# Row sums of a prompt tile in pairs of groups, between the dense blocks of a PEER layer

## What is computed

```python
def one(args):                       # 128 tokens at a time
    xb, ib, gb = args                # x, indices of 8 x 16 experts, their gates
    act = jax.nn.gelu(jnp.einsum("thkd,td->thk", u_tab[ib], xb)) * gb
    return jnp.einsum("thk,thkd->td", act, v_tab[ib])
```

## Time and profile before

| | us |
|---|---|
| median of three runs | 2733.33 |
| the profiled execution | 2734.76 |
| its span in the trace | 2733.0 |
| TensorE busy | 2637.8 (97%) |
| v products of layer 0, from the first to the last | about 995 to 1415 |
| v products of layer 1 | about 2290 to 2720 |

### The profile page before, as it was taken

How to read it: one execution, slowest core, us unless ns; L and a number is a source line. 1 busy time by engine, 2 the same in 40 slices (tenths; PEclk the granted TensorE clock), 3 DMA queues, 4 the chain that set the end, 5 groups by cost and what they waited for, 6 DMA issues and landing times. The chain is left out here.

```text
span 2733.0 us, 39630 instructions
## 1 busy us (share of the span) xinstructions
PE 2637.8 (97%) x15897; PEld 2317.3 (85%) x15897; DVE 1650.5 (60%) x3299; ACT 1035.8 (38%) x1558; POOL 713.1 (26%) x676
## 2 busy tenths in 40 slices
PE   7998799999999999999999889999999999999998
PEld 6997689999999996777779769999999999677775
DVE  3447677888344455555566568987834445555556
ACT  3444332345333332333352653334543333233332
POOL 1001200000111126776723002000011112677773
PEclk9999899999999999999999899999999999999999
DMA  8644476447798869999953123334779896999994
GB/s 302 216 154 150 153 269 218 154 170 282 277 358 310 317 246 362 377 375 384 375 202 109 63 95 115 121 141 187 281 261 355 316 316 243 358 375 386 388 371 183
DMA packets 233109, 704.65 MB, mean 258 GB/s; under 512 B 22112, under 2 KB 154592, under 8 KB 211168
## 3 DMA queue, kind: packets, MB, share of 16 engines
q1 hardware_dynamic: 172912, 516.86, 51.3%
q0 software_dynamic: 59200, 184.79, 18.6%
q10 hardware_dynamic: 816, 0.48, 0.1%
HBM read 598.12 MB, written 103.94 MB: 257 GB/s over the span
## 5 line engine op out<-in xcount | busy, mean ns | idle before, releaser
L1359 PE MATMUL hidden_ps<-h_hi,u_hi 128*128 128x384 f32 x2016 | 681.0, 338 | 2.6 <-issue 1.6
L1359 PE MATMUL hidden_ps<-h_hi,u_lo 128*128 128x384 f32 x2016 | 675.0, 335 | 0.0
L1359 PE MATMUL hidden_ps<-h_lo,u_hi 128*128 128x384 f32 x2016 | 675.0, 335 | 0.0
L2262 DVE TENSOR_TENSOR v_lo<-v_slot,v_hi 128x1024 fp32r<-128x1024 f32 x248 | 304.9, 1229 | 303.8 <-ACT v_hi L2127 302.8
L2127 ACT ACTIVATE v_hi<-v_slot 128x1024 fp32r<-128x1024 f32 x248 | 262.9, 1060 | 545.1 <-PE out_ps L2058 540.3
L2058 PE MATMUL out_ps<-v_hi,act_hi 128*128 128x512 f32 x992 | 395.7, 399 | 10.8 <-DVE act_lo L2272 10.8
L2058 PE MATMUL out_ps<-v_lo,act_hi 128*128 128x512 f32 x992 | 388.8, 392 | 0.0
L2058 PE MATMUL out_ps<-v_hi,act_lo 128*128 128x512 f32 x992 | 387.3, 390 | 0.0
L1359 PEld LDWEIGHTS hidden_ps<-h_hi,u_hi 128*128 128x128 f32 x2016 | 378.9, 188 | 4.7 <-issue 4.7
L1359 PEld LDWEIGHTS hidden_ps<-h_lo,u_hi 128*128 128x128 f32 x2016 | 379.0, 188 | 0.0
L1359 PEld LDWEIGHTS hidden_ps<-h_hi,u_lo 128*128 128x128 f32 x2016 | 378.7, 188 | 0.0
(11 more groups left out here) (502 smaller groups left out, 4009.3 us busy)
## 6 DMA issues: line engine op xcount, KB each, us to landing
u_slot<-in_peer_u SPq DMA_DIRECT2D x64, 2048.0 KB, 9.1
v_slot<-in_peer_v SPq DMA_DIRECT2D x64, 2048.0 KB, 10.2
hidden<-hidden_ring SPq DMA_DIRECT2D x64, 768.0 KB, 6.0
spread_gates<-spread SPq DMA_DIRECT2D x16, 2048.0 KB, 8.2
hidden_in<-hidden SPq DMA_DIRECT2D x64, 512.0 KB
ada_w_ring<-in_ada_w SPq DMA_DIRECT2D x48, 512.0 KB, 6.0
even_w_ring<-in_even_w SPq DMA_DIRECT2D x16, 1024.0 KB, 6.7
ada_w_ring<-in_ada_w SPq DMA_DIRECT2D x16, 1024.0 KB, 6.2
```

Source lines behind the costliest of these rows:

```text
L1359: mm = pe.matmul(PH_[:, b, 0:T], u[:, b, k * P:(k + 1) * P], x[:, k, :], start=(k == 0 and part == 0), stop=(k == KB - 1 and part == 2))
L2262: dve.tensor_tensor(lo, V[o // JC % 2][:, o % JC, :], hi.bitcast(F32), ALU.subtract).then_inc(vl, 1)
```

## The change

The row sums of two neighbouring groups are done at one place. `PAIR_AFTER[k]` = 14 + k\*108//15 for 16 pairs: 14, 21, 28, 35, 42, 50, 57, 64, 71, 78, 86, 93, 100, 107, 114, 122. Twelve of the fifteen distances are 7 blocks, three are 8. TensorE waits for the activations of both groups and for all eight rows, then does group 2k and group 2k+1 without dense work between them; each group still raises `rows_summed` by one, behind its own last matmul. VectorE makes the columns of both groups at one place too, two blocks ahead of the block (`o + 2 in PAIR_AFTER`). GpSimd's and SyncE's programs, the eleven row slots and the four activation buffers stay as they were.

```diff
-                QUAD_AFTER = [12 + i * (LATE - 14) // (QUADS - 1) for i in range(QUADS)]
+                PAIR_AFTER = [14 + i * (LATE - 16) // (QUADS // 2 - 1) for i in range(QUADS // 2)]
...
-                    def row_sums(i):
-                        pe.wait_ge(acts_made, i + 1)
-                        for j in range(4 * i, 4 * i + 4):
+                    def row_sums(pair):
+                        quads = (2 * pair, 2 * pair + 1)
+                        pe.wait_ge(acts_made, 2 * pair + 2)
+                        for j in range(8 * pair, 8 * pair + 8):
                             pe.wait_ge(slot_in[j % RING], 16 * (j // RING + 1))
-                        for c in range(2):
-                            for g in range(4):
-                                mm = pe.matmul(PO[TG * g:TG * g + TG, 0, c, :], SDW[:, i % 4, g, 31 - i:63 - i],
...
-                        mm.then_inc(rows_summed, 1)
+                        for i in quads:
+                            for c in range(2):
+                                for g in range(4):
+                                    mm = pe.matmul(PO[TG * g:TG * g + TG, 0, c, :], SDW[:, i % 4, g, 31 - i:63 - i],
...
+                            mm.then_inc(rows_summed, 1)
...
-                        if o in QUAD_AFTER:
-                            row_sums(QUAD_AFTER.index(o))
+                        if o in PAIR_AFTER:
+                            row_sums(PAIR_AFTER.index(o))
...
-                        if o + 3 in QUAD_AFTER:
-                            act_columns(QUAD_AFTER.index(o + 3))
+                        if o + 2 in PAIR_AFTER:
+                            for i in range(2):
+                                act_columns(2 * PAIR_AFTER.index(o + 2) + i)
```

More of the change, by code:

```diff
@@ L1976, in peer_experts @@
                 QUADS = P // 4
-                QUAD_AFTER = [12 + i * (LATE - 14) // (QUADS - 1) for i in range(QUADS)]
+                PAIR_AFTER = [14 + i * (LATE - 16) // (QUADS // 2 - 1) for i in range(QUADS // 2)]
                 EARLY_AFTER = {EARLY + 2 + 7 * e // 2: e for e in range(FIRST_U)}
-                assert QUAD_AFTER[-1] < LATE and max(EARLY_AFTER) < N_KEYS - 6
+                assert PAIR_AFTER[-1] < LATE and max(EARLY_AFTER) < N_KEYS - 6
                 def token(i, g):
@@ L2060, in outs @@
                         return mm
-                    def row_sums(i):
-                        pe.wait_ge(acts_made, i + 1)
-                        for j in range(4 * i, 4 * i + 4):
+                    def row_sums(pair):
+                        quads = (2 * pair, 2 * pair + 1)
+                        pe.wait_ge(acts_made, 2 * pair + 2)
+                        for j in range(8 * pair, 8 * pair + 8):
                             pe.wait_ge(slot_in[j % RING], 16 * (j // RING + 1))
-                        for c in range(2):
-                            for g in range(4):
-                                mm = pe.matmul(PO[TG * g:TG * g + TG, 0, c, :], SDW[:, i % 4, g, 31 - i:63 - i],
-                                               ROWS[(4 * i + g) % RING][:, c * CH:(c + 1) * CH],
-                                               start=(i == 0), stop=(i == QUADS - 1), skip_group_check=True)
-                        mm.then_inc(rows_summed, 1)
+                        for i in quads:
+                            for c in range(2):
+                                for g in range(4):
+                                    mm = pe.matmul(PO[TG * g:TG * g + TG, 0, c, :], SDW[:, i % 4, g, 31 - i:63 - i],
+                                                   ROWS[(4 * i + g) % RING][:, c * CH:(c + 1) * CH],
+                                                   start=(i == 0), stop=(i == QUADS - 1), skip_group_check=True)
+                            mm.then_inc(rows_summed, 1)
                     for n in range(EARLY + 1, N_KEYS):
```

## The result

The changed kernel takes 2798.54 us in the median of five runs (2793.75 to 2801.44), the kernel before 2733.33 beside it (2728.68 to 2735.05): a ratio of 1.0235 with a 95% interval of 1.0224 to 1.0247. It is slower by 65 us. The profiled execution has a span of 2792.0 us, 59.0 us more than that of before. Of all the runs told here one, a run of e2_lead0 at 2811 us, was in a slower state of the chip, and the time and the ratio of that kernel leave it out.

A forecast was written before the change was run, and what follows sets the result against it. TensorE was taken to set the time as long as it is fed. On 2734.8 us, -8.2 (saving) + 66 + 2.4 (stalls) + 6.4 (clock) gave 2801.4, with the median 1.4 lower: 2800, range 2770 to 2828.

The forecast's parts named there:

- What bounds: In the v products TensorE sets the time as long as it is fed; the DMA engines could take over.
- the saving: TensorE's row sums: a pair costs 3.83 us against 4.22 for two visits, 8.2 us gained over both layers.
- The new wait: TensorE stalls before block PA-1 while VectorE awaits gathered activations: 66 us at 7-block distances, 2.4 at 8-block ones.
- the landing as one number with a scatter: Activation gathers land 7.7 us behind issue in the middle, 16.8 us from GpSimd's release to landing.
- The clock: Halved TensorE clock behind the hole before block 13 in layer 0 and three late pairs: 6.4 us added.
- the clock falls at every stall: Rival: 38 us of slow clock in place of 4.8, or landings 1.3 us later; 2832 us, chance 0.12.
- The sum: Whole kernel: saving, stalls and clock add 66.6 us to the profiled execution's 2734.8, giving 2801.4, median 2800.
- Half of it: Rival: gathers land in 6.7 us, stalls 24 x 1.0 us less; 2774 to 2776 us, chance 0.15.
- the gathers land in time: Rival: last gather lands within 5.2 us of issue, no stall between pairs; 2727 us, chance 0.08.
- The quick landing of 2.0 us plus bytes: Skill's rule for GpSimd DMAs: gathers there at D + 13.2, no stall, time near 2728; D is the pair's start.
- a pair saves nothing: Rival: the boundary between groups costs what that to dense work costs, 12.5 us more; 2812 us, chance 0.07.
- The rows are not late: GpSimd's ninth gather behind the release lands at D + 21.7, next pair starts at D + 25.7; D is the pair's start.

The follow-up runs named there:

- e2_lead0: Changed kernel with a pair's columns made two blocks later, on another chip: 2781.1 us, ratio 1.0157 to the kernel before.
- e11: Kernel before, groups not paired, with columns made three blocks later, in the turn of their own block: 2725.59 us, ratio 0.997 to the kernel before.
- e10: Changed kernel with a pair's columns made two blocks later, in the turn of the pair's own block: 2710.79 us, ratio 0.9919 to the kernel before.
- e7: Changed kernel with the loads of v chunks 2 to 31 cut to their first block, 512 KB in place of 2 MB: 2710.77 us in one run.
- e9: Changed kernel with a pair's columns made one block later: 2722.43 us, ratio 0.9959 to the kernel before.

## Why the prediction was right, and where its terms were off

**What bounds, and the saving.** Right. 32 pairs at 3.57 us to the next dense matmul, against 1.85 + 1.72 forecast; the further semaphore waits show no cost. e11 beside e10 shows the same from the total.

**The new wait.** Right in place and in cause, too large in size. The stall lies in front of block PA-1 each time, with VectorE in `act_columns`. Where TensorE stalls, it is 2.6 us in the mean (50.1 us in 19 stalls, from the distances between its matmul starts). The 2.65 us of the forecast were meant for all 24 places with 7 blocks. Five of these have no stall at all, which makes 2.1 us for a place, and none of the six with 8 blocks has one, so the term is 50 and not 66 + 2.4 us. The columns were made 16.2 us behind the release in the mean of the 30 rounds, where I had 16.8. The step that failed is the landing as one number with a scatter. It has two kinds: at the five places without a stall the columns were made 13.0 to 14.1 us behind the release, at the 25 others 15.6 to 18.6 us. GpSimd's gathers of `picks(5)`, the columns made of them, and SyncE's loads around them:

```profile
1073.77 1.08 POOL L2177 DMA_INDIRECT row_slot<-in_peer_v,row_number  x1 [4.21 <-PE out_ps L2070]
...
1082.87 1.16 POOL L2185 DMA_INDIRECT first_act<-hidden,hidden_number  x1 [0.30 <-issue]
```
```profile
1087.82 0.17 DVE L2283 TENSOR_TENSOR act_columns<-first_act,first_picks 128x4 f32<-128x4 f32 x1 [1.81 <-DMA first_act<-hidden,hidden_number]
```
```profile
1057.89 0.33 SPq L1990 DMA_DIRECT2D v_slot<-in_peer_v  x1
...
1071.28 0.33 SPq L1990 DMA_DIRECT2D v_slot<-in_peer_v  x1
...
1085.95 0.33 SPq L1990 DMA_DIRECT2D v_slot<-in_peer_v  x1
```

These are from one of the five. Here the load of v was issued at 1071.28, 2.5 us ahead of the release, and the next at 1085.95, 12.2 us behind it. The four activation gathers, issued 5.1 to 9.1 us behind the release, fell between the two, and the last landed 4.9 us after its issue: 1.8 us of waiting, which the cover takes. For `picks(3)` a load was issued at 1057.89, 9.5 us behind the release and 0.35 us behind the last gather; that one took 7.2 us. Five pair distances, 7+7+7+7+8 = 36 blocks, are nine loads of v, so in layer 0 the early landing comes back at every fifth pair, for groups 5, 15 and 25 alike. Layer 1 agrees but for once: behind the releases at 2400.21, 2529.71 and 2663.23 the loads lie in the same way, and the columns come 13.4, 15.9 and 13.0 us behind them, the second with a stall. So the phase is not all of it. That less v traffic brings the gathers in earlier is what e7 shows; that it is the phase of the loads is read from the pattern of one trace and was not tried by itself.

**The clock.** Wrong in size: forecast 6.4 us. From the matmuls in these stretches that start 0.38 us or more (and under 0.5) apart, where 0.227 is the pace, 22.6 us are lost against 2.2 before: a term of 20.4. Of the 22.6, 16.8 lie behind the first pair of a layer, where the forecast had 4.8 in all. Layer 0's v products and one such place, as stretches with the columns of the earlier trace rows:

```profile
990.00:1445.00 455.00, 425.02 (x2063) 310.88 (x2062) 245.36 (x432) 140.18 (x135) 274.91 (x256) 0.97 0.90 330
...
1368.00:1371.20 3.20, 3.20 (x9) 2.46 (x8) 3.13 (x6) 0.00 (x0) 1.46 (x2) 0.50 0.77 210
```

The second stands behind a wait of 3.39 us and is at 1.2 GHz. I had given the fall to the few longest waits. In fact 11 of the 19 stalls have one behind them, one with only 2.0 us of standing, while one with 3.6 us has none. The length of a wait alone does not decide it. The rival in which the clock falls at every stall was more than half right.

**The sum.** -8.2 + 50.1 + 20.4 = 62.3, and the spans differ by 59.0; the 3 us between do not lie in the v products. These grew by more: from the first v product to the matmul behind the last visit 28.3 us in layer 0 and 35.9 in layer 1, 64.2 together. All that lies outside, the same work in both kernels, was 5.2 us shorter in this execution, 4.3 of it between the two layers' v products. The holes at the start are not the reason either: block 13 starts 42.8 and 42.7 us behind the first v product, before 43.3 and 43.0. Forecast were +66.6: the stalls 18 us too many, the clock 14 us too few. That the total of 2800 meets 2798.5 is luck, for two errors cancel.

**The rivals.** Two of them were half true, one in either direction. "Half of it" came nearer to the stalls than the forecast: the gathers land 6.9 us behind their issue in the middle (6.7 in the rival, 7.7 in the forecast), and the stalls are 50 us, where the rival has 44 and the forecast 68. "The clock falls at every stall" was true of 11 in 19. That the gathers land in time: no. That they would for a place of VectorE one block later: nearly, e9. The quick landing of 2.0 us plus bytes that the Trainium skill gives ("DMA: Bandwidth & Descriptors", section "Anatomy of one DMA — SWDGE (gpsimd) path") isn't reached even in e7, where the middle is 4.4 us and the least 2.3. That a pair saves nothing: no, the next dense matmul comes 3.57 us behind its start, not 4. The rows are not late: e10, with no stall between pairs, leaves them least time, and TensorE has no wait for them there.

## What to carry to other kernels

When work is put together to save its entry and exit, the semaphores that it raises are put together too: look at what they release, how far ahead of its use that lands, and what stands in the queue of the engine that waits for it. An engine that feeds the bottleneck should come to a foreign operand as late as its own consumer allows; here one line of place was worth more (80 us) than the change itself (8 to 14 us). And read a landing time with the phase of the transfers beside it, not as one number.

## What the runs showed of the hardware

- Sixteen fp32 matmuls of 128x32 by 128x512 in four column strips cost 1.72 us behind others of their kind, and 2.11 us between dense 128x128 ones.
- The granted clock fell to 1.2 GHz behind 11 of 19 stalls of 1.4 to 4.4 us, and not by their length alone: behind one of 2.0 us, and not behind one of 3.6.
- A gather of 128 numbers, 512 bytes in all, landed 4.2 to 11.3 us behind its issue while the DMA engines are some 90% busy, and in 2.3 to 7.9 us with the v loads cut to a quarter.
- The kernel before took 2732 to 2734 us in four groups of runs and 2746 us, with a wider scatter, in the fifth, on a chip that none of the other groups of experiments used; the same code (e10, e2) is faster beside it in one group (0.992) and slower in the other (1.016).
